# A hybrid decoder step on one core: the expert loop turned token-major, with eight neighbouring weight rows on each partition

## The reference

```python
logits = x @ w_router + b_router                  # 32 experts
top_v, top_i = lax.top_k(logits, 4); gates = softmax(top_v)
gu = xb @ w_gu[e] + b_gu[e]                       # 1024 x 2048 for each expert
gate, up = jnp.split(gu, 2, axis=-1)
gate = jnp.minimum(gate, 7.0); up = jnp.clip(up, -7.0, 7.0)
glu = gate * jax.nn.sigmoid(1.702 * gate)
y = ((up + 1.0) * glu) @ w_dn[e] + b_dn[e]        # 1024 x 1024, weighted by the gate and added up
```

## Time and profile before

| | |
|---|---|
| median of 3 runs | 1680.03 us (1678.45 to 1680.22) |
| span of the profiled execution | 1677.8 us; its own time outside the profile is not listed |
| PE busy | 1514.8 us (90%), weight loads 871.8 us |
| DVE, ACT, POOL busy | 449.4, 257.7, 21.9 us |
| moved by DMA | 489.80 MB in 240473 packets, mean 292 GB/s |

### The profile page before, as it was taken

How to read it: one execution, slowest core, us unless ns; L and a number is a source line. 1 busy time by engine, 2 the same in 40 slices (tenths; PEclk the granted TensorE clock), 3 DMA queues, 4 the chain that set the end, 5 groups by cost and what they waited for, 6 DMA issues and landing times.

```text
span 1677.8 us, 18682 instructions
## 1 busy us (share of the span) xinstructions
PE 1514.8 (90%) x7103; PEld 871.8 (52%) x7103; DVE 449.4 (27%) x1090; ACT 257.7 (15%) x437; POOL 21.9 (1%) x37
## 2 busy tenths in 40 slices
PE   7999999894987889899998998998988989999987
PEld 5888887652775764344343343443443443443434
DVE  2620032677134222122121122121221221211212
ACT  3113112201121111111111111111111111111112
POOL 0000000020000000000000000000000000000000
PEclk8999999896998859999999999999999999999999
DMA  5544443173237808999999999999999999999992
GB/s 178 201 150 150 150 150 134 61 236 138 101 137 262 302 0 331 387 387 387 387 387 387 387 387 387 387 387 387 387 387 387 387 387 387 387 387 387 387 387 98
DMA packets 240473, 489.80 MB, mean 292 GB/s; under 512 B 7891, under 2 KB 9835, under 8 KB 240429
## 3 DMA queue, kind: packets, MB, share of 16 engines
q1 hardware_dynamic: 237068, 478.08, 77.9%
...
HBM read 481.41 MB, written 8.19 MB: 292 GB/s over the span
## 4 chain that ended last, share of the span: by engine, by line
PE 67%; DMA 20%; DVE 8%; SPq 2%; issue 2%; ACT 1%; DVEq 0%; ACTq 0%
PE bank L1071 64%; DMA ring<-in_w_gate_up 18%; PE bank L1080 3%; SPq L371 2%; DMA projT<-in_state_ssm 2%; DVE projT L925 1%; DVE projT L1059 1%; DMA out<-projT 1%; DVE xnT L687 1%; DVE rinv L685 0%; DVE conv L884 0%; DVE projT L814 0%; DVE projT L862 0%; DVE projT L866 0%; DVE projT L864 0%
## 5 line engine op out<-in xcount | busy, mean ns | idle before, releaser
L1071 PE MATMUL bank<-ring,projT 128*64 128x512 f32 (+1 forms) x2112 | 464.5, 599 | 34.6 <-DMA ring<-in_w_gate_up 23.3
L1071 PEld LDWEIGHTS bank<-ring,projT 128*64 128x64 f32 (+1 forms) x2112 | 165.1, 137 | 301.5 <-issue 282.3
L1071 PE MATMUL bank<-flat,projT 128*64 128x512 f32 (+1 forms) x552 | 261.1, 631 | 46.6 <-DMA conv<-in_w_gate_up 46.6
L438 ACT ACTIVATE projT<-bank 128x512 f32<-128x512 f32 (+3 forms) x227 | 119.1, 529 | 1159.9 <-PE bank L1071 1153.4
L1071 PE MATMUL bank<-xnT,ring 128*128 128x264 f32 x1152 | 258.4, 388 | 3.1 <-DVE xnT L687 3.1
L1071 PE MATMUL bank<-conv,projT 128*64 128x512 f32 x512 | 250.5, 647 | 0.0
L1071 PEld LDWEIGHTS bank<-xnT,ring 128*128 128x128 f32 x1152 | 219.9, 191 | 41.3 <-issue 3.5
L1071 PE MATMUL bank<-projT 128*128 128x128 f32 (+3 forms) x1136 | 230.2, 336 | 10.3 <-DVE flat L829 2.4
L1022 DVE TENSOR_TENSOR projT<-bank,par 128x512 f32<-128x512 f32 x64 | 44.2, 691 | 625.3 <-PE bank L1080 625.3
L1071 PEld LDWEIGHTS bank<-projT 128*128 128x128 f32 (+2 forms) x1136 | 159.1, 190 | 85.8 <-DVE projT L1059 23.9
L1071 PEld LDWEIGHTS bank<-flat,projT 128*64 128x64 f32 (+1 forms) x552 | 83.3, 154 | 202.3 <-issue 200.8
...
## 6 DMA issues: line engine op xcount, KB each, us to landing
...
```

The costliest lines, as they stand in the source:

```text
L438: return s.activation(out, in_, ACT.Copy, scale=scale)
L1071: last[0] = pe.matmul(out, lhsT, rhs, start=start, stop=stop)
```

## The change

Token t's features are split over partitions as d = 8 p + k in place of 128 k + p. A chunk of gate and up weights then holds two whole neighbouring rows of 2048 for each partition (16 KB in one run, partitions 64 KB apart), and one of the down weights four whole rows of 1024 (16 KB, 32 KB apart). The sizes of the chunks, their number and their order over the slots stay. To match, `gather` and the transposes of the SwiGLU result read their stationary operand with a step of eight elements (`by_row`).

Since a stage now holds two k-blocks of all 2048 columns, the four gate and up stages add up in four banks. The bias comes in as the first product of each bank (`onehot` x `bgu`, 32 rows each), the SwiGLU runs token-major on [128 slots, 512] after the fourth stage, and only its result is transposed (8 transposes, copied by ACT). The scatter yields token-major tiles of 512 columns, six products, added to `acc` by DVE; it is done one iteration later, after the first stage. The down bias is the first scatter. The norm before the experts is folded away: `xnT` holds h times the gain, the reciprocal root is applied to the logits and in `selT`, and `xtok` holds h itself. The final norm is computed token-major.

```diff
-        wgu = a["w_gate_up"][0].rearrange("e (k p) n -> e p k n", p=P)
-        wdn = a["w_down"][0].rearrange("e (k p) n -> e p k n", p=P)
+        wgu = a["w_gate_up"][0].rearrange("e (p k) n -> e p k n", p=P)
+        wdn = a["w_down"][0].rearrange("e (p k) n -> e p k n", p=P)
...
+        def chunk_view(i, j):
+            flat_slot = mslot[i].rearrange("p k n -> p (k n)")
+            return flat_slot.rearrange("p (k n) -> p k n", k=2 if j < 8 else 4)
+        def moe_src(j):
+            w, m, k0 = (wgu, 2, 2 * (j // 2)) if j < 8 else (wdn, 4, 4 * (j // 2 - 4))
+            return w[:, :, k0:k0 + m, :]
         def moe_chunk(pair, j):
-            w, c = (wgu, j // 2 * CW) if j < 8 else (wdn, (j // 2 - 4) * CW)
-            return w[bass.ds(pair * 2 + j % 2, 1), :, :, c:c + CW].rearrange("e p k n -> (e p) k n")
+            return moe_src(j)[bass.ds(pair * 2 + j % 2, 1)].rearrange("e p k n -> (e p) k n")
...
+                    sp.dma_start(gmoe[:], a["norm_moe"][0].rearrange("(p k) -> p k", k=KB)).then_inc(S["bias_in"], 16)
+                    for q in range(4):
+                        sp.dma_start(bgu[32 * q:32 * q + 32, :], a["b_gate_up"][0][:, q * CW:q * CW + CW])\
+                            .then_inc(S["bias_in"], 16)
...
-            for j, name, k in ((2, "so", 3), (3, "so", 3), (4, "o", 3), (0, "xo", 3), (1, "xo", 7), (5, "h2ss", 0)):
+            for j, name, k in ((2, "so", 3), (3, "so", 3), (4, "o", 3), (0, "xo", 3), (1, "xo", 7), (5, "xo", 7)):
                 filled(sp, name, k)
-                sp.dma_start(mslot[j], moe_chunk(0, j)).then_inc(moe_full[j], 16)
+                if j == 4:
+                    sp.dma_start(gfin, a["norm_final"].partition_broadcast(P)).then_inc(S["gfin_in"], 16)
+                sp.dma_start(chunk_view(j, j), moe_chunk(0, j)).then_inc(moe_full[j], 16)
...
+            for i, t in enumerate((2, 0, 1)):
+                sp.wait_ge(S["y_ready"], i + 1)
+                dst = outs[1].rearrange("b s n -> (b s) n") if t == 2 else outs[0][0, t * P:(t + 1) * P, :]
+                sp.dma_start(dst, acc[0:TILES[t][1], t, :]).then_inc(S["y_out"], 16)
...
+            pool.memset(ytok, 0.0).then_inc(S["scr_zero"], 1)
+            pool.memset(gT, 0.0).then_inc(S["scr_zero"], 1)
+            for t, (_, n) in enumerate(TILES):
+                emptied(pool, "xtok", 3 + t)
+                pool.tensor_copy(acc[0:n, t, :], xtok[0:n, t, :]).then_inc(S["acc_set"], 1)
...
-            square_h("xo")
-            root("h2ss", rinv[:], T)
+            s.activation(small[:, 300:301], eps[:], ACT.Sqrt)
+            for k in range(KB):
+                emptied(s, "xo", k)
+                s.activation(sqo[:, k, :], hT[:, k, :], ACT.Square).then_inc(S["h_squared"], 1)
+                copy(xnT[:, k, :], hT[:, k, :], pcol(NMOE + k)).then_inc(S["hg_ready"], 1)
+            b = filled(s, "rt")
+            s.wait_ge(S["rr_one"], 1)
+            s.activation(rr[:, 0:2], b[:, 96:98], ACT.Sqrt, bias=eps[:, 0:1], scale=1.0 / D).then_inc(S["rr_root"], 1)
+            s.activation(rr[0:TS, 2:3], b[0:TS, 98:99], ACT.Sqrt, bias=eps[0:TS, 0:1], scale=1.0 / D)\
+                .then_inc(S["rr_root"], 1)
...
+                for h in range(2):
+                    s.wait_ge(S["g_ready"], it * 2 + (h + 1))
+                    s.activation(sig[:, h, :], gate[:, h, :], ACT.Sigmoid, scale=ALPHA).then_inc(S["sig_ready"], 1)
+                for h in range(2):
+                    s.wait_ge(S["turned"], it * 2 + (h + 1))
+                    copy(actT[:, 4 * h:4 * h + 4, :], bank[h][:, :].rearrange("p (k n) -> p k n", k=4))\
+                        .then_inc(S["actT_ready"], 1)
+                s.wait_ge(S["stage_done"], it * 6 + 6)
+                for h in range(2):
+                    copy(ytok[:, 512 * h:512 * h + 512], bank[6 + h][:, :]).then_inc(S["ytok_ready"], 1)
...
+            for i, t in enumerate((2, 0, 1)):
+                n = TILES[t][1]
+                s.wait_ge(S["tile_done"], i + 1)
+                st(s.activation(xtok[0:n, t, :], acc[0:n, t, :], ACT.Square, accum_out=rfin[0:n, t:t + 1]))
+                s.activation(rfin[0:n, t:t + 1], rfin[0:n, t:t + 1], ACT.Sqrt, bias=eps[0:n, 0:1], scale=1.0 / D)\
+                    .then_inc(S["f_rms"], 1)
...
-            add_to_h("xo")
-            norm("h2ss", xnT, hT, rinv[:], T, NMOE, "xn_ready")
+            for k in range(KB):
+                b = filled(v, "xo", k)
+                done(v.tensor_tensor(out=hT[:, k, :], in0=b[:, 0:T], in1=hT[:, k, :], op=ALU.add))
+                if k:
+                    v.wait_ge(S["h_squared"], 8 + k + 1)
+                    ins = v.tensor_tensor(out=rinv[:], in0=rinv[:] if k > 1 else sqo[:, 0, :], in1=sqo[:, k, :],
+                                          op=ALU.add)
+                    if k < KB - 1:
+                        st(ins)
+            ins.then_inc(S["sq_summed"], 1)
...
+            def ranked(dst, e0):
+                return v.tensor_tensor(out=slots_of(dst), in0=ranks, op=ALU.is_equal,
+                                       in1=rkp[:, :, bass.ds(e0, 2)].unsqueeze(3).to_broadcast([P, 3, 2, CAP]))
+            def select(e0):
+                st(ranked(selT, e0))
+                v.tensor_tensor(out=selT, in0=selT, in1=bc(rr[:, 0:3], P), op=ALU.mult).then_inc(S["sel_ready"], 1)
...
+            def spread(n):
+                for h in range(2):
+                    v.wait_ge(S["xy_full"], n + (h + 1))
+                    v.tensor_tensor(out=xg[:, 4 * h:4 * h + 4, :], in0=bank[4 + h][:, :].rearrange("p (k n) -> p k n", k=4),
+                                    in1=bc(gmoe[:, 4 * h:4 * h + 4], P), op=ALU.mult)\
+                        .then_inc(S["xg_ready"], 1)
...
+            def accumulate(it, j):
+                t, h = order[j]
+                r = TILES[t][1]
+                v.wait_ge(S["scat_full"], it * 6 + (j + 1))
+                dst = acc[0:r, t, 512 * h:512 * h + 512]
+                return v.tensor_tensor(out=dst, in0=bank[6 + j % 2][0:r, :], in1=dst, op=ALU.add)\
+                    .then_inc(S["scat_read"], 1)
...
+                v.wait_ge(S["xy_full"], it * 2 + 2)
+                select(it * 2 + 2)
+                v.wait_ge(S["gt_full"], it + 1)
+                st(ranked(selG, it * 2))
+                v.tensor_tensor(out=slots_of(selG), in0=slots_of(selG), op=ALU.mult,
+                                in1=gts[:, :, bass.ds(pair * 2, 2)].unsqueeze(3).to_broadcast([P, 3, 2, CAP]))\
+                    .then_inc(S["selg_ready"], 1)
+                v.wait_ge(S["stage_done"], it * 6 + 1)
+                v.tensor_copy(onehot.rearrange("p (j c) -> p j c", j=2),
+                              bc(id4[:, bass.ds((it + 1) % PAIRS * 2, 2)], CAP)).then_inc(S["onehot_ready"], 1)
+                for j in range(6):
+                    accumulate(it, j)
+                v.wait_ge(S["stage_done"], it * 6 + 4)
                 for h in range(2):
+                    v.tensor_scalar(gate[:, h, :], bank[h][:, :], LIMIT, None, ALU.min).then_inc(S["g_ready"], 1)
                 for h in range(2):
+                    st(v.tensor_scalar(up[:, h, :], bank[2 + h][:, :], LIMIT, -LIMIT, ALU.min, ALU.max))
+                    st(v.scalar_tensor_tensor(out=up[:, h, :], in0=up[:, h, :], scalar=1.0, in1=gate[:, h, :],
                                               op0=ALU.add, op1=ALU.mult))
                     v.wait_ge(S["sig_ready"], it * 2 + (h + 1))
+                    v.tensor_tensor(out=up[:, h, :], in0=up[:, h, :], in1=sig[:, h, :], op=ALU.mult)\
+                        .then_inc(S["act_ready"], 1)
+                spread(it * 2 + 2)
+                v.wait_ge(S["gt_full"], it + 2)
+                v.tensor_copy(gT, bank[4][:, 0:T]).then_inc(S["gT_ready"], 1)
...
+            def finish(i):
+                t = (2, 0, 1)[i]
+                r = TILES[t][1]
+                v.wait_ge(S["f_rms"], i + 1)
+                st(v.reciprocal(rfin[0:r, t:t + 1], rfin[0:r, t:t + 1]))
+                v.scalar_tensor_tensor(out=acc[0:r, t, :], in0=acc[0:r, t, :], scalar=rfin[0:r, t:t + 1],
+                                       in1=gfin[0:r, :], op0=ALU.mult, op1=ALU.mult).then_inc(S["y_ready"], 1)
+            end = n * PAIRS + PAIRS
+            for i in range(3):
+                for j in (2 * i, 2 * i + 1):
+                    accumulate(end, j)
+                v.wait_ge(S["scat_read"], end * 6 + (2 * i + 2))
+                v.memset(small[:, 310 + i:311 + i], 0.0).then_inc(S["tile_done"], 1)
+                if i:
+                    finish(i - 1)
+            finish(2)
...
-            project("xo", CH["w_xo"], oT, None, 0, "h2ss", 8)
-            pe.wait_ge(S["xn_ready"], 16)
+            project("xo", CH["w_xo"], oT, None, 0)
             b = free_bank(pe, "rt")
             for t, (c, n) in enumerate(TILES):
                 for k in range(KB):
+                    pe.wait_ge(S["hg_ready"], k + 1)
```

(74 more changed lines are left out.)

266 lines of the change are left out of this document (77 added, 189 removed).

## The result

The changed kernel takes 1714.13 us (median of 4 runs, 1709.25 to 1717.94) where the kernel before took 1680.12 beside it (4 runs, 1678.45 to 1680.73). The ratio is 1.0202, with a 95% interval from 1.0183 to 1.0221: it is 2% slower, clear of the noise. The forecast was 1589 us, the range 1568 to 1680. The profiled execution has a span of 1707.3 us.

A forecast was written before the change was run, and what follows sets the result against it. Transfers set the pace before; after, PE (60.2 us) and transfers (57.7 to 60.8) were nearly equal bounds, 60.5 an iteration. Loop -60.7, head -21.8, end -8.4 sum to -90.9: from 1680.0 to 1589 us, range 1568 to 1680.

The forecast's parts named there:

- the price of the gather: Expert loop, PE: the same 24 calls at 8.4 us an iteration, if the step of eight costs nothing.
- granted clock: Loop: expected at 2.4 GHz throughout, as PE now seldom stands still; the first iteration partly lower, 2.5 us with first bias.
- Rival 1: Gather and transposes: strided loads take longer, 3.6 to 6.2 us an iteration, 1645 to 1686 us; 12%, plus 8% beyond before.
- The transfers: Expert loop: runs of 16 KB raise 387 GB/s to 414 to 436, or 60.8 to 57.7 us an iteration.
- rival 2: Expert loop: the transfers stay at 387 GB/s, time 1647 us; chance 13%.
- rival 3: Expert loop: transfers get slower with partitions 64 KB apart, passing the time of before at 374 GB/s; chance 7%.
- PE's other pieces: Loop besides the gather: stages 42.6 us, bias 1.3, scatter 5.4, transposes, copy wait and hand-overs; PE's sum with gather 60.2.
- bias: Loop, PE: four new products an iteration, running nearly side by side as tiles of the array, 1.3 us.
- rival 4: Loop, PE: bias products go one after the other, or equal waits elsewhere, 2.2 us more, time 1620 us; chance 15%.
- scatter: Loop, PE: six calls of 512 columns at 0.87 us plus entry, 5.4 us, without a stall.
- vector chain: Loop, VectorE: eight SwiGLU operations after the fourth stage, 5.5 us, hidden by the gather's 8.4 us.
- The head and the end: Outside the loop: loop starts at 602 instead of 623.84 (-21.8 us); the end takes 14.3 instead of 22.7 (-8.4).

The follow-up runs named there:

- packed_gather: The changed kernel with xtok stored block by block, so the gather reads packed columns; the transposes keep the step of eight: 1566.78 us.
- two_blocks: The changed kernel with only the first two of the gather's eight blocks read with the step of eight, the other six packed: 1686.38 us.
- runs_2kb: The changed kernel with weight rows on partitions as before, no read with a step, every run cut to 2 KB: 1651.26 us.
- packed_both: As packed_gather, and the last SwiGLU operation writes block by block, so the transposes read packed columns too: 1562.08 us.

## Why the prediction was wrong

**The step that failed** is the price of the gather: "the same 24 calls, 8.4, if a stationary operand read with a step of eight costs nothing". It costs 15.81 us where 8.4 were put. Packing that one operand gives back 147 us, from 1714.13 to 1566.78, while the forecast was 1589. With it fell the sentence that the granted clock would stay at 2.4 GHz throughout: the argument was that PE seldom stands still, and PE did not stand still, yet the clock fell in every iteration and stayed down for 17 us (13.7 in the first).

**Rival 1 had the slower loads and not the clock.** Its price for slower loads was 3.6 to 6.2 us an iteration. Measured at the full clock it is 1.81 - 1.05 = 0.76 for each of eight blocks, 6.1 us, at its upper end. In part that is luck: the rival put 0.111 on each of 56 loads, measured were 0.13 on each of 48, and next to nothing on the eight of the transposes. But the measured loss is 68.24 - 58.87 = 9.4 us an iteration, and it adds up from three rows: gather 15.81 - 8.51 = 7.3, transposes 1.97 - 1.16 = 0.8, down stage 8.65 - 7.09 = 1.6, less the 0.25 us of a wait for ACT's copy that packed_gather has and the change has not. The loads alone, at the full clock, would have given about 1567 + 16 x 6.1 = 1665 us by this estimate, still faster than before; no kernel here shows that state, because wherever strided blocks of the gather were run the clock fell. The two costs do not simply add up: once the clock is down, the step costs only 2.03 - 1.87 = 0.16 us a block, and the lower clock 1.87 - 1.05 = 0.82. two_blocks shows how much a few loads are enough for: a quarter of the strided loads brings 7.5 of the 9.4 us. The chance of 8% for a time beyond that of before was too small for a case for which a rule spoke, and against which stood only the guess that the gather's records leave room.

**The transfers** were right: 57.7 to 60.8 us an iteration forecast, 59.1 measured (426 GB/s), and neither rival 2 nor rival 3 came about. The 16 KB packet was put at 603 ns in the best case; in the window above 1041 of them (1169 less 128 small ones) moved in 40 us on 16 engines, 615 ns each with the small ones left out.

**PE's other pieces** were right within a few tenths: bias 1.07 (from 1009.89 to 1010.96) against 1.3, so the four products do run side by side and rival 4 falls; scatter 5.6 against 5.4; vector chain 5.5, hidden. The sum without the strided operand was 1.4 too high, 58.8 measured against 60.2, since one stage follows another after 6.87 to 7.02 us where 7.1 was put, 0.8 less over six, and the waits between pieces came to 0.25 instead of 1.0. With the operand packed, the period is 58.8 us, PE and transfers at their limit together.

**The head and the end**: loop start 599.5 against 602, end 14.8 against 14.3. The first gather started 3.8 us earlier than forecast (582.54 against 586.3) and took 16.11 us where 15.03 was put, 1.1 more and not the 3 of rival 1: but for its first 1.4 us it runs at the lower clock, where the step costs little. runs_2kb lies 31 us under the kernel before that ran beside it (1651.26 against 1682.34), and 30.2 were forecast for head and end, but that the two agree is luck: its loop starts at 595.3, 28.6 us earlier than before, its end is 8 us shorter, and its loop lasts 5 us longer (1036 against 1031).

**The balance.** Forecast against measured for the change: loop 970.5 against 1093 us (599.5 to 1692.5), 122.5 more; head and end 2 us better; and the span lies 6.8 us under the median here where the forecast took 2.2, 4.6 more, since the profiled execution is the fastest of the four. That is the miss of 125 us. The 122.5 are themselves a difference: the three pieces that the step and the clock stretch cost 16 x 9.4 = 150 us, and the rest of the iteration came out 1.6 us under the 60.5 that were forecast, some 26 us in all.

What stays open: why a transpose's load costs only 0.015 us more with the step of eight (0.97 us for eight loads in packed_gather, 0.85 in packed_both) and a product's 0.12, and what in the strided loads brings the clock down. That they do bring it down is shown, by taking them out and putting them in; how is not.
